# The second weight panel three loads earlier, and a product cut in three between the transposes

## The reference, cut to what matters

```python
def rmsnorm(x, w):
    xf = x.astype(jnp.float32)
    y = xf * lax.rsqrt(jnp.mean(xf * xf, axis=-1, keepdims=True) + EPS)
    return (y * w.astype(jnp.float32)).astype(x.dtype)
...
    h = rmsnorm(x, norm_mix)
    proj = h @ w_in
    qkv_in = jnp.concatenate([conv_qkv_buf.astype(proj.dtype), proj[..., OFF_QKV:OFF_A]], axis=1)
    qkv = jax.nn.silu(causal_dwconv(qkv_in, w_conv_qkv))
```

## Time and profile before

| what | value |
|---|---|
| time, median of 3 runs | 1451.26 us (1449.9 to 1454.22) |
| profiled execution, its own time | 1451.63 us |
| its span, first to last instruction | 1449.9 us |
| PE busy | 1420.9 us, 98% of the span |
| PEld busy | 1395.5 us, 96% |
| DVE busy | 708.5 us, 49% |
| ACT busy | 478.7 us, 33% |
| POOL busy | 197.3 us, 14% |

### The profile page before, as it was taken

How to read it: one execution, slowest core, us unless ns; L and a number is a source line. 1 busy time by engine, 2 the same in 40 slices (tenths; PEclk the granted TensorE clock), 3 DMA queues, 4 the chain that set the end, 5 groups by cost and what they waited for, 6 DMA issues and landing times.

```text
span 1449.9 us, 25561 instructions
## 1 busy us (share of the span) xinstructions
PE 1420.9 (98%) x9798; PEld 1395.5 (96%) x9798; DVE 708.5 (49%) x1299; ACT 478.7 (33%) x878; POOL 197.3 (14%) x256
## 2 busy tenths in 40 slices
PE   7999999999999999999999999999999999999997
PEld 7999999999999999999999999999999999999996
DVE  5678846866837436333343333333333333344625
ACT  6324355334244226331221312203112032144525
POOL 3200211324135331000000000000000000140303
PEclk9999999999999999999999999999999999999999
DMA  7112414221223541111111111111111111112103
GB/s 184 46 44 59 103 54 140 77 76 60 59 92 72 117 90 34 55 44 44 44 46 55 45 45 44 44 43 44 57 46 44 44 44 44 44 44 74 36 24 120
DMA packets 166319, 89.88 MB, mean 62 GB/s; under 512 B 50764, under 2 KB 160268, under 8 KB 166231
## 3 DMA queue, kind: packets, MB, share of 16 engines
q1 hardware_dynamic: 165222, 84.89, 21.1%
q0 software_dynamic: 1008, 3.79, 0.6%
HBM read 77.97 MB, written 10.69 MB: 61 GB/s over the span
## 4 chain that ended last, share of the span: by engine, by line
PE 64%; DVE 2%; issue 1%; ACT 0%; DMA 0%; DVEq 0%; POOL 0%; SPq 0%
PE pg L739 63%; DVE act_lo L2036 1%; DMA out<-y_tok 0%; PE bk L1174 0%; DVE y_tok L2120 0%; PE bk L1104 0%; ACT act_hi L1193 0%; ACT sq L1193 0%; DVE xres L2160 0%; PE bk L1119 0%; DVE tm L2157 0%; ACT L1193 0%; DVE xres L2045 0%; PE bk L1165 0%; DVE tm L2146 0%
## 5 line engine op out<-in xcount | busy, mean ns | idle before, releaser
L739 PE MATMUL pg<-act_hi,w_hi 128*128 128x352 f32 x1320 | 428.5, 325 | 9.4 <-issue 3.9
L739 PE MATMUL pg<-act_lo,w_hi 128*128 128x352 f32 x1320 | 424.6, 322 | 0.0
L739 PE MATMUL pg<-act_hi,w_lo 128*128 128x352 f32 x1296 | 416.9, 322 | 0.0
L739 PEld LDWEIGHTS pg<-act_hi,w_hi 128*128 128x128 f32 x1320 | 248.7, 188 | 12.7 <-issue 6.3
L739 PEld LDWEIGHTS pg<-act_lo,w_hi 128*128 128x128 f32 x1320 | 249.3, 189 | 0.0
L739 PE MATMUL pg<-u_hi,w_hi 128*128 128x352 f32 x768 | 249.3, 325 | 0.0
L739 PE MATMUL pg<-u_hi,w_lo 128*128 128x352 f32 x768 | 248.9, 324 | 0.0
L739 PE MATMUL pg<-u_lo,w_hi 128*128 128x352 f32 x768 | 247.8, 323 | 0.0
L739 PEld LDWEIGHTS pg<-act_hi,w_lo 128*128 128x128 f32 x1296 | 244.1, 188 | 0.0
L1193 ACT ACTIVATE w_hi<-w_raw 128x1024 fp32r<-128x1024 f32 x111 | 117.2, 1056 | 357.3 <-PE pg L739 320.1
L2097 DVE TENSOR_TENSOR xres<-xres,pg 128x352 f32 (+1 forms) x192 | 99.2, 520 | 201.4 <-PE pg L739 201.4
(11 more groups left out here) (344 smaller groups left out, 1478.8 us busy)
## 6 DMA issues: line engine op xcount, KB each, us to landing
w_raw<-in_w_up SPq DMA_DIRECT2D x32, 512.0 KB, 4.0
w_raw<-in_w_down SPq DMA_DIRECT2D x32, 512.0 KB, 3.3
w_raw<-in_w_in SPq DMA_DIRECT2D x29, 512.0 KB, 3.9
x_tok<-in_x_prompt SPq DMA_DIRECT2D x8, 512.0 KB, 7.6
w_raw<-in_w_out SPq DMA_DIRECT2D x8, 512.0 KB, 4.2
x_col<-in_x_prompt SPq DMA_DIRECT2D x32, 128.0 KB, 2.7
w_raw<-in_w_ple_gate SPq DMA_DIRECT2D x8, 512.0 KB, 4.0
out<-y_tok SPq DMA_DIRECT2D x8, 512.0 KB, 3.3
```

Of the source, the lines that this page charges most:

```text
L739: last = mm(pg[bank][:, 0:TH], w, a, start=i == 0, stop=i == len(terms) - 1)
```

## The change

The panel of the first unit is loaded behind the fourth tile of x (tile 3), and not behind the last tile and the two states. ACT and DVE split it two tiles earlier: ACT after tile 3 in place of tile 5, DVE after tile 4 in place of tile 6. `first_group(0)` is cut in three parts of 8 matmuls, one behind the turns of each of the tiles 5, 6 and 7; the second `ab_group` follows the last part. All three `ab_group` now use the bank `pg2`, so the second waits until the first is copied out, and `first_group(1)` goes ahead of the third `ab_group`. The first unit's thirds are moved out of PSUM by plain copies, without waiting for the norm; DVE then multiplies the whole row of 1,056 by the norm in place (`first_norm`), and POOL's `keep_state(1)` waits for that.

```diff
@@ SP
                 if t == 1:
                     load_w(0, 0, win_v[:, :, OFF_A:OFF_A + P], KD)
+                if t == 3:
+                    load_in(U_QKV)
             sp.dma_start(st_in[:, :], ...
             sp.dma_start(sc_in[:, :], ...
-            load_in(U_QKV)
@@ PE
             def ab_group(n):
+                if n > 0:
+                    pe.wait_ge(sm.ab_kept, n)
                 terms = [(w_hi[0][:, k, :], a[:, k, cols(n)]) for k in range(KD) for a in (act_hi, act_lo)]
-                products(n, terms).then_inc(sm.ab_mm, 1)
-            def first_group(n):
-                pe.wait_ge(sm.ab_kept, n + 1)
-                products(n, parts(1, KD, 0, act_hi, act_lo, n)).then_inc(sm.mm_done, 16 if n == 0 else 4)
+                products(2, terms).then_inc(sm.ab_mm, 1)
+            def first_group(n, a=0, e=3 * KD):
+                if n == 2:
+                    pe.wait_ge(sm.ab_kept, 3)
+                for i, (w, m) in enumerate(parts(1, KD, 0, act_hi, act_lo, n)):
+                    if a <= i < e:
+                        last = mm(pg[n][:, 0:TH], w, m, start=i == 0, stop=i == 3 * KD - 1)
+                if e == 3 * KD:
+                    last.then_inc(sm.mm_done, 16 if n == 0 else 4)
...
+                if t == 4:
                     panel_ready(0, 0)
-                    ab_group((t - 4) // 3)
+                    ab_group(0)
+                elif t in (5, 6, 7):
+                    panel_ready(U_QKV, 0)
+                    first_group(0, (t - 5) * KD, (t - 4) * KD)
+                if t == 7:
+                    ab_group(1)
...
-            panel_ready(U_QKV, 0)
-            first_group(0)
+            first_group(1)
             pe.wait_ge(sm.xlo_even, NTT + 1)
             pe.wait_ge(sm.xlo_odd, NTT + 1)
             ab_group(2)
-            first_group(1)
             pe.wait_ge(sm.r_chain, 5)
@@ ACT
-                if t in (1, 5):
-                    split_w((t - 1) // 4, 0)
+                if t in (1, 3):
+                    split_w((t - 1) // 2, 0)
@@ DVE
-                if t in (2, 6):
-                    split_w((t - 2) // 4, 0)
+                if t in (2, 4):
+                    split_w((t - 2) // 2, 0)
...
+            def first_third(n):
+                a, e = n * TH, min(n * TH + TH, TP)
+                product_ready(U_QKV, 0, 4 * n + 4)
+                last = nc.vector.tensor_copy(pre[0][:, PAD + a:PAD + e], pg[n][:, 0:e - a])
...
+            def first_norm():
+                dve.wait_ge(sm.r_chain, 9)
+                dve.wait_ge(sm.evacuated, 12 * U_QKV + 12)
+                now = pre[0][:, PAD:PAD + TP]
+                link(tt(now, now, r_b[:, 0:TP], MUL))
+                now = samples(pre[0])[:, :, PAD:SEG]
+                link(tt(now, now, r_b[:, TP:T].rearrange("p (b t) -> p b t", t=NT), MUL))
...
-            dve.wait_ge(sm.r_chain, 9)
+            dve.wait_ge(sm.state_put, U_QKV)
+            for n in range(3):
+                first_third(n)
+            first_norm()
@@ POOL, keep_state
+                if b == U_QKV:
+                    pool.wait_ge(sm.chain, 2)
```

More of the change, by code:

```diff
@@ L456, in ab_tokens @@
             return flat(LY[0])[:, 0:NPAR * AB].rearrange("p (t c) -> p t c", t=NPAR)
-        CHAIN_ABS, CHAIN_LOG_A, CHAIN_BETA, CHAIN_G = 3, 20, 22, 24
+        CHAIN_ABS, CHAIN_LOG_A, CHAIN_BETA, CHAIN_G = 5, 22, 24, 26
         PARAMS = 16 * (6 + CW + SW)
@@ L1632, in ab_rows @@
                     dve.wait_ge(sm.x_squared, 2)
-                nc.vector.tensor_copy(qkv[0:AB, 0, cols(n)], pg[n][0:AB, 0:TH]).then_inc(sm.ab_kept, 1)
+                nc.vector.tensor_copy(qkv[0:AB, 0, cols(n)], pg[2][0:AB, 0:TH]).then_inc(sm.ab_kept, 1)
             dve.wait_ge(sm.gain_in, 16)
@@ L1671, in to_columns @@
                 return last
+            def first_third(n):
+                a, e = n * TH, min(n * TH + TH, TP)
+                product_ready(U_QKV, 0, 4 * n + 4)
+                last = nc.vector.tensor_copy(pre[0][:, PAD + a:PAD + e], pg[n][:, 0:e - a])
+                if n == 2:
+                    last = nc.vector.tensor_copy(samples(pre[0])[:, :, PAD:SEG],
+                                                 pg[n][:, e - a:TH].rearrange("p (b t) -> p b t", t=NT))
+                last.then_inc(sm.evacuated, 16 if n == 0 else 4)
+            def first_norm():
[5 more added lines that the diff above has]
+                link(tt(now, now, r_b[:, TP:T].rearrange("p (b t) -> p b t", t=NT), MUL))
             def qkv_third(b, n):
@@ L1677, in qkv_third @@
                 product_ready(b, 0, 4 * n + 4)
-                to_columns(pre[(b - 1) % 2], n).then_inc(sm.evacuated, 16 if b == U_QKV and n == 0 else 4)
+                to_columns(pre[(b - 1) % 2], n).then_inc(sm.evacuated, 4)
             def tap(b, w):
@@ L1755, in decays @@
                 ts_(eneg[:, :, :], eneg[:, :, :], -1.0, None, MUL).then_inc(sm.gl_made, 1)
-            dve.wait_ge(sm.r_chain, 9)
+            dve.wait_ge(sm.state_put, U_QKV)
+            for n in range(3):
+                first_third(n)
+            first_norm()
             dve.wait_ge(sm.params_in, PARAMS)
             for b in range(U_QKV, U_F):
-                for n in range(3):
-                    qkv_third(b, n)
+                if b > U_QKV:
+                    for n in range(3):
+                        qkv_third(b, n)
                 unit_done(b, 0)
```

## The result

Over 20 executions of each kernel on the same chip, the changed kernel takes 1455.12 us in the median (1452.39 to 1457.93) and the kernel before 1450.82 (1449.36 to 1454.22). The ratio is 1.0029, with a 95% interval of 1.0022 to 1.0036: slower by 4.3 us. In a later session, with 11 and 30 executions, it was 3.9 us and 1.0023 (1.0014 to 1.0032). The change costs about 0.3%. The kernel before measured against itself gave 0.9 us (experiment 11), so the 4 us are real, and a difference of 1 us or less can't be told from none.

What follows compares the result with a forecast made beforehand. It took the ninth tile and the norm chain of 10.24 us behind it to bound the opening, not PE's holes. 1.15 + 0.25 + 1.5 = 2.9 us gave 1454.2 us, range 1451.0 to 1457.0.

Steps and rivals of the forecast that it cites:

- The late ninth tile: Opening: blocked `w_lo` takes 2.31 us, ninth tile's gain comes at 30.0 instead of 28.85, norm matmuls start 1.15 us later.
- The multiply in place: First unit's eviction: the separate norm multiply adds 1.6 us on DVE; PE waits 0.25 us at the third unit.
- One fall of the clock on the path: Opening, behind one of PE's two idle times: the clock falls once, costing 1.5 us; chance 0.38.
- The first idle time: PE behind the turns of tile 5: a new wait of some 2.5 us, until `w_lo` ends at 21.3.
- The idle time before the norm matmuls: PE behind the third `ab_group`: there at 37.7, it idles 2.5 us until the norm matmuls at 40.25.
- The load, at 0: Second panel, issued at about 4.2 us, lands at 11 to 13; costs 0, at most 1.5 us.

Runs made afterwards that it cites:

- experiment 11: The kernel before, unchanged, measured again against itself: 1450.41 us against 1451.33, ratio 0.9996.
- experiment 1: The changed kernel with DVE's second-panel `w_lo` one place earlier, ahead of `act_lo` of tile 4 and POOL's part: 1453.00 us against 1451.46 for the kernel before.
- experiment 3: The changed kernel with the first unit's thirds again multiplied by the norm as they leave PSUM: 1454.69 us, ratio 1.0029 to the kernel before.
- experiment 2: The changed kernel with 14 unused matmuls on PE ahead of the norm matmuls: 1453.13 us, ratio 1.0011 to the kernel before.
- experiment 10: The changed kernel with only the second panel's load moved behind tile 4 instead of tile 3: 1456.01 us, ratio 1.0033 to the kernel before.
- experiment 6: The changed kernel with the third `ab_group` ahead of `first_group(1)` and the squares of tiles 4 and 5 earlier: 1451.23 us against 1450.73 for the kernel before.
- experiment 4: The changed kernel with the third `ab_group` ahead of `first_group(1)` again: 1454.05 us, ratio 1.0022 to the kernel before.
- experiment 8: The changed kernel with `w_lo` ahead of `act_lo` of tile 4, third `ab_group` ahead of `first_group(1)`, two squares earlier: 1450.17 us against 1450.73 for the kernel before.
- experiment 7: The kernel before with the squares of tiles 4 and 5 moved earlier, nothing else: 1450.16 us against 1450.73, ratio 1.0000.
- experiment 5: The changed kernel with 12 unused matmuls ahead of the `w_lo` wait and 14 ahead of the norm matmuls: 1451.87 us against 1450.73 for the kernel before.

## Why the prediction was right, step by step

The prediction was 1454.2 us with a range of 1451.0 to 1457.0; 1455.12 was measured (1455.23 in the later session). The sum of its terms, 2.9 us, is what the one profile shows at the second unit; that this profile had just the one fall of the clock that was forecast is luck in part: the second profile of the changed kernel had a longer one, and that of experiment 1 none.

- **The late ninth tile, 1.15 us.** Right. `w_lo` 2.30 us at 18.90 (2.31 and 18.9 predicted); the gain at 30.08 (30.0); from there to the norm matmuls 10.28 us (10.24); norm matmuls at 40.36 (40.25). By the Trainium skill, "SBUF — State Buffer", section "Who interferes with whom", a DVE instruction with two SBUF inputs contends with a GpSimd instruction that reads SBUF, and issue order decides which of them blocks. The traces agree for both orders. Where POOL was first by 0.05 us, `w_lo` took 2.30, and away from POOL 1.22 (experiment 1). The 1.1 us that the prediction gave as left of POOL's instruction is 1.22 by its own rows (24.60 plus 1.26, less 24.64), so the sum is 2.4 for a measured 2.31. And at 51.05 in the changed kernel, where DVE started a `w_lo` first, POOL's copy was the one that took long: 1.24 us for three columns, against 0.21 for the 24 behind it:

```profile
51.05 1.23 DVE L1622 TENSOR_TENSOR w_lo<-w_raw,w_hi 128x1024 fp32r<-128x1024 f32 x1
```
```profile
51.08 1.24 POOL L2249 COPY st_O<-pre 128x3 f32<-128x3 f32 x1 [4.05 <-DVE pre L1702]
52.27 0.21 POOL L2250 COPY st_O<-pre 128x24 f32<-128x24 f32 x1
```

- **The multiply in place, 0.25 us.** Right: 1.23 and 0.19 us on DVE, 0.22 at the third unit, and experiment 3 finds nothing that its 6 executions could tell.
- **One fall of the clock on the path, 1.5 us.** Right in the profile: 1.63 us, behind the second idle time. Experiment 2 shows the cause by filling it. But the fall doesn't come every time: five profiles have 2.50 or 2.51 us of idle time there, and the clock fell in four (the changed kernel's two, experiments 3 and 10) and held in one (experiment 1). The first idle time brought no fall in the changed kernel's two profiles, where it was 2.06 and 1.35 us, nor with 2.07 in experiment 6; with 2.34 us in experiment 10 it did.
- **The idle time before the norm matmuls, 2.5 us.** The size was right, 2.51. The reason was half of it, so the right size is partly luck. I had PE early and one chain late. The second chain is the third `ab_group`, its copy on DVE and the reciprocal behind it: the swap with `first_group(1)` put 3.84 us of matmuls in front of it. It was in the order of the queues and I did not follow it. In the changed kernel both end within 0.05 us. So repairing one alone gives little: experiment 4, with the copy out of the way, still has the norm at 40.44. (The squares alone were not tried in the changed kernel.) Experiment 1, which leaves both, keeps the 2.51 us. Both repairs together, experiment 6, take the norm matmuls to 37.98.
- **The load, at 0.** Right in the first profile, too simple in the others. The panel was issued at 5.09, not 4.2, and took 8.3 us, so it landed at 13.4, well before ACT wants it at 15.6:

```profile
w_raw<-in_w_in SPq DMA_DIRECT2D x1, 512.0 KB, 8.3
```

I argued that a tile of x may come 2 us late since PE stands at the `w_lo` wait anyway. The tile did come late (its turns start at 14.66, before at 13.70). But the wait of 0.84 us lies in the first burst of turns. PE starts at the lower clock level (eight turns took 1.97 us there and 1.10 later) and the clock rises somewhere before 20 us. In the nine profiles with the load behind tile 3, it was up for good at 13.5 to 15.0 in three and at 18.2 to 19.6 in six. In the five without, it was up by 15.1 each time. If the load had no part in it, all six late ones would fall among the nine in about 3 of 100 draws (84 of 3003). The pattern was noticed in these same profiles, and only the last four were taken after it, so the load's part is likely and not shown. A late rise makes the turns of tile 4 0.9 us and the `ab_group` 0.9 to 1.5 us longer. In the changed kernel's order most of it hides under the wait for `w_lo`: with a late rise the ninth tile was turned at 30.40 in its second profile and at 30.02, 29.49 and 29.70 in the experiments 2 to 4, against 29.61 with the early rise. So the term was 0.8 us at most and near 0 in the rest.
- **From profile to median.** The sum of 2.9 us stands against 4.3 and 3.9 measured. The mean clock of every execution helps here. Twice the missing share of the clock, times the execution's time, gives 13.2 us at half clock for the kernel before (88 executions, standard error 0.4) and 16.0 us for the changed one (31, 0.6). The time before the clock's first rise isn't in it. Each lost microsecond at half costs at most 0.5. The opening's fall is in both kernels, free in one, on the path in the other. The surplus of 2.8 us (standard error 0.7) is worth up to 1.4, by this estimate: second or longer falls in some openings, and the longer stretch near the end, may be what it is made of. Chain 1.27, third unit 0.22 and fall 1.63 make 3.1, and with the surplus up to 4.5, around the 4.05 between the two means. It is a rough account: of the 2.9 us at the second unit 2.7 were left by 1300, so the third unit's 0.22 doesn't show there.

What stays open is the end. The stretch of 10.24 us at half clock stands in both profiles of the changed kernel and in those of the experiments 2 and 10, not in that of experiment 3, whose opening is the same, and the tail's code differs in none. The last 100 matmuls and what follows them took 24.65 and 24.57 us in two profiles of the kernel before, 26.84 and 27.35 in those of the changed one, and 23.91 in experiment 3. The length goes with where the low clock sets in. In the four profiles with the long stretch it begins 8.8 to 9.4 us behind the start of those 100 matmuls; in nine others 7.6 to 8.6 us, with a first stretch of 3.4 us, and in experiment 8 at 13.0, with 6.8. Whether the change moves the tail to the worse place or it falls there by chance, no run was made to tell.

## What to carry to other kernels

Work moved into an engine's idle time delays all that stands behind it in that queue; ask which chain hangs on that, and whether it is the one that ends last. Where two chains arrive together, shortening one moves little (experiments 4 and 7), so follow each back through every queue before a change is priced. And an idle time that costs nothing as a wait may cost through the clock behind it, here 1.6 us for 2.5 us idle. Cheap filler work is the test (experiment 2), as long as it can't outlast the wait that it fills (experiment 5).

## What the runs showed of the hardware that was not expected

- When the clock rises is not fixed by the kernel: at 13.4 and 13.9 us in two profiles of the kernel before, at 13.5 in one of the changed kernel, and in the other at 8.0, down again at 11.4, and up at 18.3. In experiment 7 it rose at 8.75 and fell at 22.4. An idle time of 0.7 to 1.1 us ahead of tile 4 stands in all six profiles with a late rise, and in three without.
- The same idle time of 2.5 us before the norm matmuls was followed by a fall of the clock for 3.4 us (three profiles) or 6.8 us (one), or by none (experiment 1).
- Useless matmuls made a kernel faster: 14 of them, 2.4 us of PE's time, took 1.6 to 2.6 us off the difference to before.
- Executions of one kernel spread over some 5 us (1448.4 to 1453.7 in 88), and the slower ones had the lower mean clock: the correlation between an execution's time and its time at half clock was 0.64 to 0.73 in the three sessions of the kernel before (0.31 in the 11 executions of experiment 11), and 0.68 and 0.86 in the two of the changed one. One profile shows one draw of this.
